# High and low halves of the values in one stationary: eight attention-value products a unit in place of twelve

## What is computed

```
p = exp(s - m)
denom = sum(p) + exp(sink - m)
o = einsum('bckgqj,bcjkd->bcqkgd', p / denom, v)      # k: 2 value heads, g: 8 query heads each, d: 64
m = sigmoid(gate_A) * o + sigmoid(gate_B) * conv      # merged branches, then @ w_out
```

## Time and profile before

| | |
|---|---|
| median of 3 runs | 3257.81 us (3253.9 to 3260.78) |
| the profiled execution | 3250.26 us, span 3248.2 us |
| TensorE busy | 3166.5 us, 97% of the span |
| TensorE's mean granted clock | 0.992 |
| VectorE, ScalarE, GpSimd busy | 47%, 33%, 16% |

### The profile page before, as it was taken

One profiled execution on the slowest core, in us unless ns is written; L12 is line 12 of the kernel. 1 busy time (PEld: TensorE's weight loads), 2 busy tenths in 40 slices (PEclk: granted clock), 3 DMA queues, 4 the chain that ended last, 5 costly groups with the idle time before them and its releaser, 6 DMA issues.

```text
span 3248.2 us, 42967 instructions
## 1 busy us (share of the span) xinstructions
PE 3166.5 (97%) x17053; PEld 2698.5 (83%) x17053; DVE 1533.0 (47%) x2729; ACT 1064.9 (33%) x1905; POOL 505.9 (16%) x543
## 2 busy tenths in 40 slices
PE   7989989999999999999999999999999999999998
PEld 6768878878877878888887888888899898899987
DVE  7977655544876631003495652002388555200013
ACT  5666432234446420003255522002234542200012
POOL 4830000000561000000183000000057100100000
PEclk9999999999999999999999999999999999999999
DMA  8854667777553355555654344555454332444443
GB/s 280 293 215 175 235 231 287 290 277 286 212 180 128 118 206 181 189 194 201 219 186 153 121 179 168 194 188 207 177 203 175 123 118 106 163 178 177 174 155 125
DMA packets 176487, 622.68 MB, mean 192 GB/s; under 512 B 20656, under 2 KB 26672, under 8 KB 175776
## 3 DMA queue, kind: packets, MB, share of 16 engines
q1 hardware_dynamic: 175328, 619.53, 52.8%
q10 hardware_dynamic: 960, 0.40, 0.0%
HBM read 480.41 MB, written 139.54 MB: 191 GB/s over the span
## 4 chain that ended last, share of the span: by engine, by line
PE 80%; ACT 2%; DVE 2%; DMA 1%; POOL 1%; issue 1%; SPq 0%; DVEq 0%; POOLq 0%; ACTq 0%
PE PS L790 52%; PE PS L842 7%; PE PS L844 7%; PE PS L843 7%; PE PS L824 2%; PE PS L931 2%; PE PS L919 1%; POOL sq_sum L732 1%; PE PS L950 1%; PE PS L951 1%; PE PS L952 1%; PE PS L969 1%; PE PS L771 1%; DVE PS L1474 1%; ACT act_hi L1246 0%
## 5 line engine op out<-in xcount | busy, mean ns | idle before, releaser
L790 PE MATMUL PS<-h_hi,w_hi 128*128 128x512 f32 (+1 forms) x3328 | 1065.6, 353 | 13.4 <-DVE u L1705 4.8
L790 PE MATMUL PS<-h_hi,w_lo 128*128 128x512 f32 (+1 forms) x3328 | 1066.1, 353 | 0.0
L790 PE MATMUL PS<-h_lo,w_hi 128*128 128x512 f32 (+1 forms) x3328 | 1055.6, 350 | 0.0
L790 PEld LDWEIGHTS PS<-h_hi,w_hi 128*128 128x128 f32 x3328 | 586.2, 189 | 96.4 <-issue 18.5
L790 PEld LDWEIGHTS PS<-h_lo,w_hi 128*128 128x128 f32 x3328 | 585.9, 189 | 90.8 <-issue 2.2
L790 PEld LDWEIGHTS PS<-h_hi,w_lo 128*128 128x128 f32 x3328 | 586.6, 189 | 81.3
L1474 DVE SCALAR_TENSOR_TENSOR PS<-u,dw,PS 128x512 f32<-128x512 f32 (+1 forms) x604 | 434.0, 765 | 7.0
L726 POOL TENSOR_TENSOR y<-y,prod 128x512 f32<-128x512 f32 (+1 forms) x333 | 402.8, 1235 | 192.5 <-ACT prod L1224 180.8
L1860 DVE TENSOR_TENSOR f<-PS,tmp 128x512 f32<-128x512 f32 (+1 forms) x88 | 61.5, 699 | 670.8 <-PE PS L790 652.1
L842 PE MATMUL PS<-w_hi,f_hi 128*128 128x512 f32 x748 | 298.1, 399 | 5.8 <-DVE f L1860 5.4
L844 PE MATMUL PS<-w_hi,f_lo 128*128 128x512 f32 x748 | 295.6, 395 | 0.0
(11 more groups left out here) (193 smaller groups left out, 3648.4 us busy)
## 6 DMA issues: line engine op xcount, KB each, us to landing
w_lo<-lo_dram SPq DMA_DIRECT2D x372, 512.0 KB, 4.4
w_hi<-hi_dram SPq DMA_DIRECT2D x372, 512.0 KB, 3.4
w_raw<-in_w_stream SPq DMA_DIRECT2D x124, 512.0 KB, 3.9
hi_dram<-w_hi SPq DMA_DIRECT2D x124, 512.0 KB, 4.0
lo_dram<-w_lo SPq DMA_DIRECT2D x124, 512.0 KB, 3.9
x<-in_x_prompt SPq DMA_DIRECT2D x4, 2048.0 KB, 12.1
xs<-in_x_prompt SPq DMA_DIRECT2D x12, 512.0 KB, 5.4
out_y_prompt<-x SPq DMA_DIRECT2D x3, 2048.0 KB, 10.6
```

What stands on the lines that cost most here:

```text
L790: last = nc.tensor.matmul(PS[:, k0 + off, 0:n], w, x[:, k, c0:c0 + n], start=first and k == 0, stop=stop and k == KT - 1)
```

## The change

The value tiles become one, `v_all`, with `[v0 high, v0 low, v1 low, v1 high]` side by side. A 128-column slice of it is a stationary with high and low part of one head, so one matmul by the high probabilities gives high by high in one half of the partitions and low by high in the other. The product of the high values by the low probabilities needs 64 columns only. The two heads now lie in two banks (6 and 7), both used by every output, and a new tile `attended` takes the sum of the two halves.

```
-        v_hi = at("v_hi", room(7 * 3 * HD * 4), [P, 7, 3, HD], F32R)
-        v_lo = at("v_lo", room(7 * 3 * HD * 4), [P, 7, 3, HD], F32R)
+        v_all = at("v_all", room(7 * 4 * HD * 4), [P, 7, 4, HD], F32R)
+        attended = at("attended", room(4 * P * 4), [P, 4 * P])
...
             def times_values(b, n):
-                if hp == 0 and o >= 2:
-                    pe.wait_ge(o_out, o - 1)
+                if hp == 0 and gu >= 2:
+                    pe.wait_ge(o_out, gu // 2)
                 for kt in range(2):
...
-                    out = PS[:, 6 + o % 2, hp * 2 * P:(hp + 1) * 2 * P]
+                    c = slice(hp * 2 * P, (hp + 1) * 2 * P)
                     for kv in range(2):
...
-                        nc.tensor.matmul(out, vh, ph, start=kv == 0 and kt == 0, stop=False)
-                        nc.tensor.matmul(out, vh, pl, start=False, stop=False)
-                        last = nc.tensor.matmul(out, vl, ph, start=False, stop=kv == 1 and kt == 1)
+                        products = [(PS[:, 6 + kv, c], both, ph), (PS[0:HD, 6 + kv, c], v_all[r, vt, 3 * kv, :], pl)]
+                        for i, (out, vx, px) in enumerate(products if kt == 0 else products[::-1]):
+                            last = nc.tensor.matmul(out, vx, px, start=kt == 0 and i == 0, stop=kt == 1 and i == 1)
```

ScalarE copies the half that lies in the other head's partitions (before `probs_hi` of the same iteration), and VectorE adds:

```
+            def low_values(b, o):
+                go = U0[b] // 2 + o
+                n = KT * S if PAIRS[o][1] == 4 else 4 * P
+                act.wait_ge(pv_done, min(2 * go + 2, U0[b] + units(b)))
+                if go:
+                    act.wait_ge(o_out, go)
+                A(attended[0:HD, 0:n], PS[HD:P, 6, 0:n], ACT.Copy)
+                A(attended[HD:P, 0:n], PS[0:HD, 7, 0:n], ACT.Copy).then_inc(low_out, 1)
...
             def gated_out(b, o):
+                n = KT * S if tt == 4 else 4 * P
+                dve.wait_ge(low_out, go + 1)
+                for kv in range(2):
+                    rows_of = slice(HD * kv, HD * kv + HD)
+                    ins = TT(attended[rows_of, 0:n], PS[rows_of, 6 + kv, 0:n], attended[rows_of, 0:n], ALU.add)
+                link(ins)
...
-                src = PS[:, 6 + go % 2, :].rearrange("p (h t) -> p h t", h=4)
+                src = attended[:].rearrange("p (h t) -> p h t", h=4)
                 STT(q[:, *part], gates[:, *part], 1.0, src, ALU.add, ALU.mult).then_inc(o_out, 1)
```

At step 50 the fourth token tile of the output projection goes into bank 6, which the last output still holds in block 0. Its wait for that output moves there from step 54 (the tiles now go in the order 0, 1, 2, 3, before it was 0, 1, 3, 2), and in block 0 the last `gated_out` comes before the merging in VectorE's list:

```
                         if s == S_W and kk == 0 and tt == 2:
                             pe.wait_ge(pt_lo_ok, U0[b] + units(b))
+                        if s == S_W and kk == 0 and tt == 3:
+                            pe.wait_ge(o_out, U0[b] // 2 + outputs(b))
```

More of the change, by code:

```diff
@@ L218, in build @@
         sbias_in = sem("sbias_in")
+        low_out = sem("low_out")
         yn_ok, ahi_ok, afull_ok, alo_ok = sem("yn_ok"), sem("ahi_ok"), sem("afull_ok"), sem("alo_ok")
@@ L704, in _ @@
             nc.gpsimd.memset(u_hist[:], 0.0).then_inc(setup_ok, 1)
-            nc.gpsimd.memset(v_hi[:].bitcast(F32), 0.0).then_inc(setup_ok, 1)
-            nc.gpsimd.memset(v_lo[:].bitcast(F32), 0.0).then_inc(setup_ok, 1)
+            nc.gpsimd.memset(v_all[:, 0, :, :].bitcast(F32), 0.0).then_inc(setup_ok, 1)
             nc.gpsimd.memset(k_hi[:, 0:P].bitcast(F32), 0.0).then_inc(setup_ok, 1)
@@ L709, in _ @@
             nc.gpsimd.memset(pss[:], 1.0).then_inc(setup_ok, 1)
-            pool.wait_ge(setup_ok, 8)
+            pool.wait_ge(setup_ok, 7)
             for tt in range(4):
@@ L938, in times_values @@
                 gu = U0[b] + n
-                o = gu // 2
                 pe.wait_ge(pt_lo_ok, gu + 1)
-                if hp == 0 and o >= 2:
-                    pe.wait_ge(o_out, o - 1)
+                if hp == 0 and gu >= 2:
+                    pe.wait_ge(o_out, gu // 2)
                 for kt in range(2):
                     vt, r = (6, 5)[kt] if tt == 4 else tt + kt, slice(0, S if tt == 4 and kt else P)
-                    out = PS[:, 6 + o % 2, hp * 2 * P:(hp + 1) * 2 * P]
+                    c = slice(hp * 2 * P, (hp + 1) * 2 * P)
                     for kv in range(2):
-                        vh, vl = (v[r, vt, :, :].rearrange("p a d -> p (a d)")[:, kv * HD:kv * HD + P]
-                                  for v in (v_hi, v_lo))
+                        both = v_all[r, vt, 2 * kv:2 * kv + 2, :].rearrange("p a d -> p (a d)")
                         ph, pl = (px[r, kt, kv * 2 * P:(kv + 1) * 2 * P] for px in (pt_hi, pt_lo))
-                        nc.tensor.matmul(out, vh, ph, start=kv == 0 and kt == 0, stop=False)
-                        nc.tensor.matmul(out, vh, pl, start=False, stop=False)
-                        last = nc.tensor.matmul(out, vl, ph, start=False, stop=kv == 1 and kt == 1)
+                        products = [(PS[:, 6 + kv, c], both, ph), (PS[0:HD, 6 + kv, c], v_all[r, vt, 3 * kv, :], pl)]
+                        for i, (out, vx, px) in enumerate(products if kt == 0 else products[::-1]):
+                            last = nc.tensor.matmul(out, vx, px, start=kt == 0 and i == 0, stop=kt == 1 and i == 1)
                 last.then_inc(pv_done, 1)
@@ L985, in _ @@
             pe.wait_ge(ident_in, 16)
-            pe.wait_ge(setup_ok, 8)
+            pe.wait_ge(setup_ok, 7)
             for tt in range(4):
@@ L1056, in _ @@
                             result_out(pe, b, S_W - 1)
-                            pe.wait_ge(o_out, U0[b] // 2 + outputs(b))
                         if s == S_W and not ext(b):
-                            token_major(b, s, S_W, h_hi, h_lo, (2 * i, 2 * i + 1), HALF_W, (0, 1, 3, 2))
+                            token_major(b, s, S_W, h_hi, h_lo, (2 * i, 2 * i + 1), HALF_W, range(4))
                             if left_open(b):
@@ L1272, in _ @@
             act.dma_start(ckv[:, 1, :], cache_v).then_inc(const_in, 16)
-            act.wait_ge(setup_ok, 8)
+            act.wait_ge(setup_ok, 7)
             sum_squares(0, 0, 0)
@@ L1351, in _ @@
                         for n in units_at(b, s):
+                            if 3 <= n <= units(b) + 1 and n % 2 == 1:
+                                low_values(b, (n - 3) // 2)
+                            if ext(b) and n == units(b) + 1:
+                                low_values(b, outputs(b) - 1)
                             if 0 < n <= units(b):
@@ L1367, in _ @@
                     if s == S_W:
+                        if gated_late(b):
+                            low_values(b, outputs(b) - 1)
                         if left_open(b):
@@ L1379, in _ @@
                                 A(kx[:, 0:P], kx[:, T:T + P].bitcast(F32), ACT.Copy)
-                            for vx in (v_hi, v_lo):
-                                ins = A(vx[:, 0, 0:3:2, :], vx[:, 4, 0:3:2, :].bitcast(F32), ACT.Copy)
-                            ins.then_inc(hist_ok, 1)
+                            A(v_all[:, 0, :, :], v_all[:, 4, :, :].bitcast(F32), ACT.Copy).then_inc(hist_ok, 1)
                     if ext(b) and s == S_W + HALF_W:
@@ L1650, in masks @@
                     link(nc.vector.memset(part, NEG))
-            dve.wait_ge(setup_ok, 8)
+            dve.wait_ge(setup_ok, 7)
             scale_rows(0, 0, 0)
@@ L1674, in _ @@
             TT(ck_lo[:], ckv[:, 0, :], ck_hi[:].bitcast(F32), ALU.subtract)
[L1675 to L1676 removed]
+            TT(v_all[:, 6, 1:3, :], ckv[:, 1, :].rearrange("p (a d) -> p a d", a=2),
+               v_all[:, 6, 0:4:3, :].bitcast(F32), ALU.subtract).then_inc(cache_ok, 1)
             for b in range(NB):
@@ L1815, in _ @@
                     if s == S_W:
+                        if gated_late(b):
+                            gated_out(b, outputs(b) - 1)
                         for t in MERGES[b][s - 1]:
```

20 lines of the change are left out of this document (9 added, 11 removed).

## The result

The changed kernel took 3279.66 us (median of 4 runs, 3272.53 to 3285.53) against 3257.41 of the kernel before (4 runs): ratio 1.0067, 95% interval [1.0054, 1.0079]. It is slower by 22 us; forecast was 4, with a range that ended at 3276.

A forecast was written before the change was run, and what follows sets the result against it. TensorE, 80% of the chain, was taken as the bound. Blocks gave +8.0 (block 0), +0.8 (1 and 2), -4.7 (3): +4.1 on 3257.8, so 3262, range 3249 to 3276; of 31 us saved, 35 waited back.

The forecast's parts named there:

- the place of the new wait: Odd iterations from 3: TensorE waits for the queries' low part before the scores, 1.2 in blocks 1 and 2.
- even iterations 0.50 shorter in gate steps: Iterations without gating and queries: four fewer value products at 0.12 each shorten them by 0.48.
- no wait in block 3's conv steps: Block 3's conv steps, 11.49 long before, still take 11.0, which covers the 9.66 until the next scores.
- the wait for an output at step 50 of block 0: Fourth token tile waits for the last output, whose gating ends at 4.05 against TensorE's 2.1: +2.0.
- half the partitions cost as much as all: Copies and additions on 64 partitions are priced like 128: two copies 1.09, two additions 1.28.
- the maxima start at t + 3.1 ... 1.0 late: Block 1's odd iterations: copies and additions delay VectorE's maxima from 2.07 to 3.1 after t, the scores' start.
- rival (3): Larger hand-overs, passed on whole in 26 iterations: all of 0.25 plus one slow clock gives +13, 3271; 30%.
- after a wait of 2.65 nothing of it: In the earlier trace, a TensorE wait of 2.65 was taken to leave the clock at full rate.
- It decides from a wait somewhere between 2.65 and 3.60: Wait length from which TensorE's clock falls; the change's waits were put at about 20 of 1.2 to 2, one of 3.
- rival (2): Waits halve TensorE's clock, 2.5 us each: about 20 falls, +50, 3311, 5%; just one, +2.5, a third.
- (1): Gain kept: copies and additions on 64 partitions take half the time, maxima not late; 26 us less, 3231; 11%.
- (4): Value products of 64 columns cost more than 0.12; each 0.02 would be 5 us where unhidden; 3%.

The follow-up runs named there:

- experiment 2: Changed kernel without the two copies and two additions an output, the gating reading one bank: 3228.46 us, ratio 0.9915.
- experiment 11: Changed kernel with its two additions in the other order, upper 64 partitions first: 3272.75 us, ratio 1.0056.
- experiment 1: Changed kernel unedited, timed and profiled once more: 3280.02 us, ratio 1.0074.
- experiment 5: Changed kernel with only the gating moved behind the probabilities' low part, copies and additions where they were: 3252.74 us, ratio 0.9991.
- experiment 8: Kernel before, with its twelve products, plus the change's two copies and two additions an output: 3280.91 us, ratio 1.0076.
- experiment 10: Changed kernel with the fourth token tile of step 50 taken last: 3278.30 us, ratio 1.0064.
- experiment 3: Changed kernel with useless TensorE products ahead of the scores that wait for the queries' low part: 3271.62 us, ratio 1.0053.
- experiment 7: Control: kernel before, with the next pair's queries moved early and nothing else: 3252.19 us, ratio 0.9996.
- experiment 4: Changed kernel with the next pair's queries early, low part behind the probabilities' low part on VectorE: 3238.36 us, ratio 0.9946.

## Why the prediction was wrong

**Right:** what bounds the kernel, the products (0.12 each, eight a unit; experiment 2 gave back 28 of the 31), the place of the new wait, even iterations 0.50 shorter in gate steps, no wait in block 3's conv steps, the wait for an output at step 50 of block 0 (2.08, forecast 2.0), and that half the partitions cost as much as all: a copy of 64x512 took 0.59, one of 128x512 on the same engine 0.58 to 0.60.

**The first step that failed is a size: "the maxima start at t + 3.1 ... 1.0 late".** On the same clock of stamps (t = 1049.89, the end of the value products in the chain) they start at 1053.36, t + 3.47. The terms: copies 1.20 where 1.09 was taken, hand-over 0.10 for 0.03, additions 1.39 for 1.28, gating to maxima 0.72 for 0.60; only the start was 0.02 earlier. That is 0.39, and 0.06 lie between the stamps of the two views: 10.11 in place of 9.66. So the waits came out at 1.54 to 1.65, 2.05 and 1.13 where 1.2, 1.8 and 0.7 were forecast. The rows that I took the prices from are pairs of instructions on all 128 partitions, which overlap by a tenth: the two copies are 1.09, less than twice 0.60. Here both additions, 0.69 each, and both copies, 0.59 each, follow without overlap. For VectorE the Trainium skill ("VectorE: DVE Perf Modes", section on two Vector instructions with no wait between them) has the rule: an instruction that starts in another group of 32 partitions than the last one that read or wrote the same memory is held until all before it have finished. The traces agree: 1.39 for 2 x 0.69, and, in experiment 11, maxima that come 0.11 earlier when the last addition reads the group of partitions in which they start. For ScalarE's copies no experiment was made; that they follow at 0.61 is only seen. In rival (3) I had this step with 0.25 at most, for one or two hand-overs; it was 0.45 in 16 odd iterations of blocks 1 to 3, 7 us. In block 0 the copies also started later than I had them, since the gate ahead of them ended at 279.28, 0.7 after the chain's t and not 0.58. The row was there: the earlier trace rows have the gate end at 273.26 + 0.58 = 273.84, and I took 273.75. Odd iterations are 10.80 for 10.22 with n = 3, 5, 7, 9. There n = 13 was 0.7 better than forecast (the lateness of the memset had been absorbed in the longer iteration ahead of it). Net the order cost 15 in place of 4.

**The second step that failed is a mechanism: "after a wait of 2.65 nothing of it", and so "It decides from a wait somewhere between 2.65 and 3.60".** The first is a misreading, and that trace sets no such limit. The earlier trace rows show only the first product behind that wait. The granted clock fell 0.74 later, and the 24 products of which it is the first took 4.80, where the next 24 took 3.01 (the chain, kernel before):

```profile
2817.36 4.80 PE PS L824 x24
...
2823.04 3.01 PE PS L824 x24
```

Single products of 272 columns, 0.29 before the fall, are 0.43 behind it (timeline of TensorE):

```profile
2817.85 0.29 PE L824 MATMUL PS<-h_hi,w_hi 128*128 128x272 f32 x1
...
2818.31 0.43 PE L824 MATMUL PS<-h_hi,w_hi 128*128 128x272 f32 x1
```

The same profile had more that went against a limit, in both directions. A wait of 1.79 was followed by a lower clock, and one of 3.60, in n = 1 of block 2, by none (timeline of TensorE, then windows as above):

```profile
454.85 0.47 PE L790 MATMUL PS<-h_hi,w_hi 128*128 128x512 f32 x1 [1.79 <-ACT tmp L1328]
...
1778.99 1.09 PE L931 MATMUL PS<-ident_sb,p 128*128 128x128 f32 x8 [3.60 <-DVE p L1579]
```

```profile
2817.36:2822.17 4.81, 4.80 (x26) 4.81 (x27) 3.50 (x5) 1.15 (x2) 1.18 (x3) 0.65 0.33 136
454.85:459.85 5.00, 5.00 (x15) 3.96 (x16) 2.94 (x3) 1.06 (x1) 0.00 (x0) 0.66 1.01 366
1778.99:1786.98 7.99, 7.99 (x44) 6.84 (x44) 5.26 (x18) 5.60 (x13) 0.00 (x0) 1.00 0.04 8
```

So the profile of the kernel before already had a fall behind a wait under 2, and the 5% for rival (2) rested on a row read too short. Over the seven profiles that have such waits ahead of an even iteration's scores (the changed kernel, experiments 1, 2, 5, 8, 10 and 11), the even iterations behind them that ran at the lower clock were:

| wait before the scores, us | even iterations | at the lower clock |
|---|---|---|
| 0.83 to 1.40 | 50 | 0 |
| 1.44 to 1.59 | 25 | 0 |
| 1.63 to 1.65 | 24 | 12 |
| 1.73 and 1.74 | 2 | 1 |
| 2.04 to 2.07 | 24 | 22 |

It is not the wait alone: of those at 1.63 to 1.65 half went through, the same ones in all three profiles that have them, and the 3.60 above did too. What distinguishes them stays open. But that standing still is the cause is shown: experiment 3 took it away with work of no other use, and the falls went with it. Nine at 1.6 are 14 in a profile; between the profiles of experiments 1 and 3 it is 11, between their medians 8. A part of that gap is what the added products cost, and the rest isn't resolved. So, in the medians, 15 for the order and 8 for the clock make 23; 22 were measured.

**Of the rivals,** (3) came true, beyond the size that I had allowed it, and (2) in part, with 9 falls where I had given it one or some twenty. (1) is what experiment 2 shows, a gain that this order of the work doesn't keep. (4) is refuted.

**What the sum could not show:** it took the order of the work as it stands. That the queries' low part comes last on VectorE in an odd iteration cost nothing before (experiment 7), and the earlier trace rows show it there, 0.3 ahead of need. With the maxima 1.4 late it is worth some 33 us: 3271.62 with the clock held up (experiment 3) against 3238.36 with the low part moved (experiment 4).

## What to carry to other kernels

When work is taken from the bounding engine and a little of it put on another, look in each iteration at which engine's chain is the longer one afterwards: the saving counts only where it is still TensorE's, and what is added counts whole where it isn't. Then look at what the late result is queued behind, since moving it may cost nothing, as here (experiment 7). Price two instructions in a row from a pair that starts in the same partitions as yours. And price a new, repeated wait of TensorE with a fall of the clock behind it (here 35 of 50 iterations behind waits of 1.63 to 2.07 had one, at 1.6 us each), unless rows of the kernel at hand speak against it. When you look in a trace for what a wait did to the clock, read the granted clock over the microseconds that follow, not the first instruction.

## What the runs showed of the hardware

Two VectorE operations on different halves of the partitions take 1.39 where two on all 128 take 1.28, and the order of the halves moves the next instruction by 0.11. TensorE at 1.2 GHz for part of an iteration of 8.4 cost 1.6 us; it came behind waits as short as 1.63, and not behind one of 3.60. In the kernel before, the fall behind a wait of 2.65 came 0.74 after the wait's end. Useless products in a wait of 1.65 made the kernel 8 us faster.
